# Last feed-forward stage by block products: seven products in place of eight for six of its eight chunks

## What is computed

```
h2 = rmsnorm_2(x, norm_mlp_g[l])
up = jnp.square(jax.nn.relu(jnp.einsum('bsd,df->bsf', h2, w_up[l])))     # 1024 -> 4096
x = x + jnp.einsum('bsf,fd->bsd', up, w_down[l])                         # 4096 -> 1024
```

## Time and profile before

| what | us |
|---|---|
| median of 3 runs | 996.32 (995.89 to 996.4) |
| span of the profiled execution, first to last instruction | 994.1 |
| PE busy | 987.6 (99%) |
| DVE busy | 682.7 (69%) |
| ACT busy | 553.6 (56%) |
| POOL busy | 118.6 (12%) |

### The profile page before, as it was taken

The page is one execution under the profiler, slowest core; times in us unless marked ns, Lnnn a source line. Parts: engine busy times, 40 slices in busy tenths (PEclk is TensorE's granted clock), DMA queues, the critical chain, the costliest instruction groups (busy, mean ns, idle before and its releaser), DMA issues.

```text
span 994.1 us, 12539 instructions
## 1 busy us (share of the span) xinstructions
PE 987.6 (99%) x4608; PEld 810.6 (82%) x4608; DVE 682.7 (69%) x998; ACT 553.6 (56%) x761; POOL 118.6 (12%) x109
## 2 busy tenths in 40 slices
PE   8999999999999999999999999999999999999998
PEld 7788888888777788888888888888888888888887
DVE  6666566668987667656565678776689767656663
ACT  7444343577665546444444586868885555443542
POOL 0000000022300000000000041169904000000000
PEclk9999999999999999999999999999999999999999
DMA  7987776586444546766666487658555546777761
GB/s 263 284 266 255 234 250 211 193 305 196 140 152 143 169 130 214 227 198 214 211 204 226 156 229 237 176 163 212 151 191 196 202 156 204 228 223 227 226 198 43
DMA packets 165465, 201.44 MB, mean 203 GB/s; under 512 B 55969, under 2 KB 111658, under 8 KB 165290
## 3 DMA queue, kind: packets, MB, share of 16 engines
q1 hardware_dynamic: 164826, 200.69, 64.3%
q10 hardware_dynamic: 592, 0.14, 0.1%
HBM read 182.45 MB, written 5.77 MB: 189 GB/s over the span
## 4 chain that ended last, share of the span: by engine, by line
PE 96%; DVE 2%; ACT 1%; POOL 1%; issue 0%; ACTq 0%; POOLq 0%; DVEq 0%
PE bank L1969 23%; PE bank L1971 23%; PE bank L1970 23%; PE bank L2087 7%; PE bank L2086 7%; PE bank L2085 7%; PE bank L1984 1%; PE bank L2136 1%; PE bank L2251 1%; DVE lo L1348 0%; PE bank L2151 0%; PE bank L2138 0%; PE bank L2374 0%; PE bank L2375 0%; PE bank L2347 0%
## 5 line engine op out<-in xcount | busy, mean ns | idle before, releaser
L1969 PE MATMUL bank<-hi,xh 128*128 128x512 f32 (+1 forms) x944 | 374.8, 397 | 0.9 <-DVE lo L1574 0.8
L1971 PE MATMUL bank<-hi,xl 128*128 128x512 f32 (+1 forms) x944 | 367.2, 389 | 0.0
L1970 PE MATMUL bank<-lo,xh 128*128 128x512 f32 (+1 forms) x944 | 366.5, 388 | 0.0
L1331 DVE TENSOR_TENSOR lo<-raw,hi 128x2048 fp32r<-128x2048 f32 (+1 forms) x111 | 253.9, 2289 | 146.2 <-ACT hi L824 146.2
L824 ACT ACTIVATE hi<-raw 128x2048 fp32r<-128x2048 f32 (+1 forms) x114 | 216.5, 1901 | 133.7 <-PE bank L2087 97.0
L1969 PEld LDWEIGHTS bank<-hi,xh 128*128 128x128 f32 x944 | 177.3, 188 | 39.7 <-issue 2.5
L1971 PEld LDWEIGHTS bank<-hi,xl 128*128 128x128 f32 x944 | 177.2, 188 | 37.2
L1970 PEld LDWEIGHTS bank<-lo,xh 128*128 128x128 f32 x944 | 177.5, 188 | 34.4
L1348 DVE TENSOR_TENSOR lo<-raw,hi 128x1024 fp32r<-128x1024 f32 (+1 forms) x108 | 131.9, 1230 | 43.1 <-ACT hi L833 42.4
L2085 PE MATMUL bank<-hi,hh 128*128 128x512 f32 (+1 forms) x306 | 119.3, 390 | 0.0
L2087 PE MATMUL bank<-hi,hl 128*128 128x512 f32 (+1 forms) x306 | 118.7, 388 | 0.0
(11 more groups left out here) (271 smaller groups left out, 961.6 us busy)
## 6 DMA issues: line engine op xcount, KB each, us to landing
raw<-in_w_in SPq DMA_DIRECT2D x48, 1024.0 KB
raw<-in_ffn_w_gu SPq DMA_DIRECT2D x82, 512.0 KB
raw<-in_ffn_w_down SPq DMA_DIRECT2D x22, 1024.0 KB
raw<-in_w_up SPq DMA_DIRECT2D x16, 1024.0 KB
raw<-in_w_down SPq DMA_DIRECT2D x16, 1024.0 KB
raw<-in_w_out SPq DMA_DIRECT2D x8, 1024.0 KB
distance_table<-ftab SPq DMA_DIRECT2D x8, 576.0 KB
raw<-in_w_proj_attn SPq DMA_DIRECT2D x4, 1024.0 KB
```

The costliest lines, as they stand in the source:

```text
L1331: nc.vector.tensor_tensor(lo[s][:, :, 0:width], raw[s][:, :, 0:width], hi[s][:, :, 0:width].bitcast(F32), ALU.subtract).then_inc(lo_done, 1)
L1969: nc.tensor.matmul(o, sh, wh, start=first and j == 0, stop=False)
L1970: nc.tensor.matmul(o, sh, wl, start=False, stop=False)
L1971: ins = nc.tensor.matmul(o, sl, wh, start=False, stop=last and j == 3)
```

## The change

Chunks 0 and 1 are computed as before, but one directly after the other, chunk 1 into the banks X[0] and X[1]. Chunks 2 to 7 are taken as three pairs. In a pair, the up product is a 2x2 block product: rows are the two token tiles, the inner dimension is two halves of 512, and columns are the two chunks of the pair. It is computed in seven block products (`p1` to `p7`) of one unit and 12 matmuls each, where before there were four up units of 24. The formula needs sums of blocks on both sides:

- Four sums of the input, made once by POOL in `xn` (four of 128x512, after two adds of 128x1024 that rebuild the input from `xh` and `xl`), and split by ACT and DVE into `sum_h`, `sum_l`.
- Four sums of weight blocks per pair (`weight_sums`, t = 1 to 4), each one POOL instruction on 128x2048 numbers. The weights of a pair are loaded into `operand` buffers of their own, outside the ring's `raw` buffers; `hi` and `lo` are still the ring of three.
- PSUM results are kept by ACT (`keep`), further products are added onto the same bank, and DVE adds the rest (`add_product`, three per pair). The squares go to ACT (`square`). The transposes of the last chunk go by DMA as all others.

The order of PE's work in a pair is one table; "a0" to "b1" are the four down units of earlier chunks:

```diff
-UNITS = U_L + 4 * NF2
+NPAIR = (NF2 - 2) // 2
+PRODUCTS = ["p1", "p2", "a0", "p6", "a1", "p7", "p5", "b0", "p4", "p3", "b1"]
+U_PAIR = U_L + 4
+UNITS = U_PAIR + len(PRODUCTS) * NPAIR + 4
+OPERAND = {"p1": 0, "p2": 1, "p6": 5, "p7": 2, "p5": 4, "p4": 1, "p3": 3}
...
+            def last_operand(j, b):
+                half, chunk = b % 2, 2 + 2 * j + b // 2
+                if j == 0:
+                    sp_eng.wait_ge(k_rl, 2)
+                else:
+                    sp_eng.wait_ge(lo_done, product_unit(j - 1, ("p1", "p4", "p7", "p3")[b]) + 1)
+                    sp_eng.wait_ge(last.t_made, 4 * j - (3, 0, 1, 1)[b])
...
             for c in range(4):
                 for half in range(2):
                     columns(a["w_proj_attn_2" if c < 2 else "w_proj_rnn_2"], U_P2 + 2 * c + half, c % 2 * W, half)
+                    if (c, half) in ((2, 1), (3, 1)):
+                        last_operand(0, 2 * (c - 2))
...
+            for j in range(NPAIR):
+                i = 2 + 2 * j
+                if j < NPAIR - 1:
+                    last_operand(j + 1, 0)
+                last_down(i - 1, 1)
+                last_down(i, 0)
+                flip_last(i, 0, 2 * i + 1)
+                if j < NPAIR - 1:
+                    last_operand(j + 1, 2)
+                    last_operand(j + 1, 1)
+                last_down(i, 1)
+                flip_last(i, 1, 2 * i + 2)
+                if j < NPAIR - 1:
+                    last_operand(j + 1, 3)
...
+            def weight_sums(j, which):
+                def sum_up(t, left, right, op):
+                    pool.wait_ge(last.t_made, 4 * j + t - 1)
+                    nc.gpsimd.tensor_tensor(operand[(4, 5, 2, 1)[t - 1]][:, :, :], operand[left][:, :, :],
+                                            operand[right][:, :, :], op).then_inc(last.t_made, 1)
...
+            weight_sums(0, (1, 2, 3))
             norm_rstd(4)
...
+            weight_sums(0, (4,))
+            for j in range(1, NPAIR):
+                weight_sums(j, (1, 2, 3, 4))
```

DVE's part of a pair, new:

```diff
+                for j in range(NPAIR):
+                    last_split_lo(product_unit(j, "a0"))
+                    add_product(j, 0)
+                    last_split_lo(product_unit(j, "p6"))
+                    last_split_lo(product_unit(j, "a1"))
+                    last_merge(2 * j + 1)
+                    pair_planes(j, 0)
+                    last_split_lo(product_unit(j, "p7"))
+                    last_lo(2 * j + 1)
+                    last_split_lo(product_unit(j, "p5"))
+                    last_split_lo(product_unit(j, "b0"))
+                    last_split_lo(product_unit(j, "p4"))
+                    add_product(j, 1)
+                    last_split_lo(product_unit(j, "p3"))
+                    last_split_lo(product_unit(j, "b1"))
+                    pair_planes(j, 1)
+                    last_split_lo(product_unit(j, "b1") + 1)
+                    add_product(j, 2)
+                    last_merge(2 * j + 2)
+                    pair_planes(j, 2)
+                    last_split_lo(product_unit(j, "b1") + 2)
+                    pair_planes(j, 3)
+                    last_lo(2 * j + 2)
```

More of the change, by code:

```diff
@@ L192, in __init__, with own @@
         self.merged = sem(name + "_merged")
-        self.tr = sem(name + "_tr")
+    def own(self, sem, name):
+        self.g0 = sem(name + "_g0")
+        self.acted = sem(name + "_acted")
         self.hh = sem(name + "_hh")
@@ L922, in ffn_iter @@
                 split_hi(n + 4, off)
[L923 to L924 removed]
+                split_hi(n + 5, off)
             def ffn(f, width=lambda n: W):
@@ new lines, in ffn, with last_split_hi @@
+                norm(f.norm + 1, third_unit, lambda: None)
+            def last_split_hi(n):
+                if n >= UNITS:
+                    return
+                s = n % RING
+                name = PRODUCTS[(n - U_PAIR) % len(PRODUCTS)]
+                j = (n - U_PAIR) // len(PRODUCTS)
+                if j < NPAIR and name in OPERAND:
+                    if name in ("p1", "p2", "p3"):
+                        act.wait_ge(last.b_in[OPERAND[name]], 16 * j + 16)
+                    else:
+                        act.wait_ge(last.t_made, 4 * j + ("p5", "p6", "p7", "p4").index(name) + 1)
+                else:
+                    r = [r for r in range(U_PAIR, U_PAIR + 2 * NF2) if slot_unit(r) == n][0]
+                    act.wait_ge(raw_in[r % RING], UNIT_IN * (r // RING + 1))
+                act.wait_ge(used, n - 2)
+                nc.scalar.activation(hi[s][:, :, :], whole(n)[:, :, :], ACT.Copy).then_inc(hi_done, 1)
@@ new lines, in sum_hi, with keep @@
+            def sum_hi(m):
+                act.wait_ge(last.x_made, (3, 5, 4, 6)[m - 1])
+                cut = slice(4 * (m - 1), 4 * m)
+                nc.scalar.activation(sum_h[:, cut, :], x_block[m], ACT.Copy).then_inc(last.s_hi, 1)
+            def keep(j, k):
+                act.wait_ge(used, product_unit(j, ("p1", "p6", "p7")[k]) + 1)
+                if j == 0 and k == 0:
+                    act.wait_ge(last.s_lo, 4)
+                elif j > 0:
+                    act.wait_ge(last.planes, 4 * j + (1, 4, 3)[k])
+                nc.scalar.activation((c11, c12, c22)[k], G[0][:, :], ACT.Copy).then_inc(last.kept, 1)
@@ new lines, in square @@
+            def square(j, k):
+                c = (c11, c21, c22, c12)[k]
+                rstd = rstd_x[:, 0:1] if k in (0, 3) else rstd_x[:, 1:2]
+                if k == 1:
+                    act.wait_ge(used, product_unit(j, "p4") + 1)
+                    if j > 0:
+                        act.wait_ge(last.planes, 4 * j + 2)
+                    nc.scalar.activation(c, G[0][:, :], ACT.Relu, scale=rstd).then_inc(last.acted, 1)
+                    act.wait_ge(last.acted, 4 + j + 1)
+                else:
+                    act.wait_ge(last.added, 3 * j + (1, 0, 2, 3)[k])
+                    step(nc.scalar.activation(c, c, ACT.Relu, scale=rstd))
+                nc.scalar.activation(c, c, ACT.Square).then_inc(last.squared, 1)
@@ new lines, in last_ffn @@
+            def last_ffn():
+                ffn_first(last)
+                second_chunk()
+                for j in range(NPAIR):
+                    for name in PRODUCTS:
+                        if name in OPERAND:
+                            product(j, name)
+                        else:
+                            last_down(2 * j + "ab".index(name[0]), int(name[1]))
+                for i in (NF2 - 2, NF2 - 1):
+                    for b in range(2):
+                        last_down(i, b)
```

733 lines of the change are left out of this document (479 added, 254 removed).

## The result

The changed kernel takes 1060.91 us (median of 4 runs, 1054.94 to 1062.55), the kernel before 996.21. The ratio is 1.064, 95% interval 1.0612 to 1.0668. The profiled execution has a span of 1060.7 us.

What follows compares the result with a forecast made beforehand. PE, busy 99% of the span, was taken to bound the kernel. Span 994.1 less 9.0 of saved PE work plus 55.9 of waits gave 1041.0; the median lies 2.2 above, so 1043 us, range 998 to 1056.

Steps and rivals of the forecast that it cites:

- 1, late load of U_P2+6: Output projections: this unit's load is issued behind one waiting for `k_rl`, so PE waits; +3.5 us.
- 2, sums at the output projections: Output projections: POOL's t1 falls in slack, t2 and t3 of pair 0 hit the turned `otl`; 2 us taken.
- 3, chunks 0 and 1: Before a0 of pair 0: DVE's 19.2 us of work plus 13.8 inserted by POOL outlast PE's cover; +12.7 us.
- 4, pair ends: Two pair ends: three POOL sums (t2, t3, t4) enter DVE's queue; +14.7 us each, 29.4 in all.
- 5, t1 beside b0: Next pair's first weight sum runs beside the split of b0, which has 5.44 us of cover; +2.4 us twice, 4.8.
- 6, after the last pair: After the last pair no p1 and p2 cover DVE's chain of planes, split and low part; +3.5 us.
- Q: Time of one POOL sum of 128x2048, charged in DVE's queue: 4.6 us taken, between 4.4 and 5.8.
- the walk: Place-by-place count of waits; for chunks 0 and 1, DVE from 823.3 to 856.3 until a0 of pair 0 can run.
- The clock falls in the gaps: Rival: three PE gaps of 9 to 13 us each followed by a half-clock unit, 5.4 us each; about 1059; chance 0.05.
- long instructions of both engines run side by side: Rival: DVE and POOL overlap on long instructions, leaving 10.3 to 18.1 us of waits; 998 to 1005; chance 0.15.
- The 16-number row: A 3.90 us POOL instruction on 16 numbers, in whose last 0.56 us a DVE split took its undisturbed 1.23.
- Faster: Rival: PE's waits sum to less than 9.0 us, so time falls, to 987 at no wait; chance 0.10.

Runs made afterwards that it cites:

- fill experiment: The changed kernel with 174 idle matmuls into the unused bank X[1], written ahead of the waits where PE stands idle: 1050.02 us.
- free sums: The changed kernel with weight and input sums on POOL cut to 4 columns and the first operand loads of pair 0 issued later: 996.32 us.

## Why the prediction was wrong, step by step

The direction was right, and the time lay 5 us above the range. The gaps of PE, each from the end of one matmul's 0.227 us to the start of the next in PE's timeline, against the terms of the sum:

| step | forecast | measured |
|---|---|---|
| 1, late load of U_P2+6 | 3.5 | 4.7 |
| 2, sums at the output projections | 2 | 4.9 (2.4, 0.7, 1.8) |
| 3, chunks 0 and 1 | 12.7 | 9.7 (3.0, 6.7) |
| 4, pair ends | 29.4 | 27.6 (13.8 twice) |
| 5, t1 beside b0 | 4.8 | 6.0 (3.2, 2.8) |
| 6, after the last pair | 3.5 | 3.5 |
| sum | 55.9 | 56.4 |

**The cost of POOL's sums was right, and so were the places.** That the sums of the table agree within 0.5 us is luck in part: single steps are off by up to 3 us, both ways. Q = 4.6 was right: 4.62 us for a sum that DVE barely disturbed. Step 2 was too low since I named `otl`, where the sums hit `xn` and the gates as well. Step 3 was too high by 3.0. In the trace DVE takes 31.2 us from the planes at 837.86 to the end of a0's split at 869.10, where the walk had 33.0, and some 1.6 more are covered by PE itself, whose matmuls ran slow from 857.9 to 861.3. Its 3.0 us before p2 are the input sums' doing: they stay with the weight sums on few columns (2.8 in the list of waits) and are gone when the input sums are small too. Step 4 put 14.7 at each pair end and got 13.8: the sums hit the planes and the two low parts, 13.0 us in place of three times 4.6, and the split of p2 escaped. Step 5's 2.4 doesn't come out of its terms: a sum paid in full gives 1.91 + 2.29 + 4.6 - 5.44 = 3.4, which is nearer to the 3.2 and 2.8 measured.

**The step that failed is the clock.** I set the span as 994.1 - 9.0 + 55.9, every matmul at 0.227 us, and gave "The clock falls in the gaps" 0.05. Measured, 985.1 + 56.4 is 1041.5, and the span is 1060.7; 19 us are matmuls at the lower level. The granted clock says the same by itself: nine stretches at 0.5 lie behind the eleven gaps, PE works in about 37 us of them, and half of that is 18. That is the whole miss. The chance was the error: I took the absence of a lower clock in a trace whose longest wait is 1.8 us as evidence for gaps of 13 us, of which it says nothing. The price, 5.4 us for each of three gaps, was also built wrong. Behind the long gaps the matmuls of 4.9 us ran slow, which loses half of that, about 2.5; but nearly every gap had it, those of 3 us too. The window from 880 to 900, whose one gap is 3.2 us, has a granted clock of 0.91; the gap of 1.8 at 806 had no such stretch. So nine stretches cost about 2 us each, and not three 5.4. That this rival's time, about 1059, lies 2 us from the measured one is luck: 3 x 5.4 is 16.2, and 9 x 2.1 is 19. The fill experiment took 10.9 us out by this alone, down to 1050.0, inside the range. The Trainium skill, "TensorE: Matmul & The Clock Gate", section "Part 1: The HAM clock gate", has the halving of an idle PE, and this trace agrees (0.54 and 0.51 in the windows at 922 to 936.5); I cited it and then left it out of the sum.

**The rivals.** That long instructions of both engines run side by side is refuted by the sums on few columns, by one sum twice, and by the 5.08 and 9.90 us rows. The 16-number row of POOL, on which it rested, is one case in which DVE didn't wait. That such an instruction lets DVE through because it reads next to nothing, and has read it by then, is argued, not shown. The forecast for that rival, 998 to 1005 with steps 1 and 6 in place, was also a little low: the experiment with sums on few columns, input sums and late load in place, has 1009.4, and the one without these 996.3. "Faster" had its point at 9.0 us of stall in total; even with free sums the stalls and their clock make about that much (996.3, where 987.2 is the time before less 9.0).

**Open.** The runs of the changed kernel scatter by 7.6 us (1054.94 to 1062.55), those of the kernel before by 0.5; the mean clocks of the four runs (0.976 for the fastest, 0.971 for the slowest) suggest that it is the length of the slow stretches that varies, but what sets it in a run was not tried. Nor is a gap's price the same each time: behind the last gap of 3.5 us the changed kernel lost 1.7 us and the version with free sums 3.0, and in the fill experiment a gap of 3.0 at 854 had none (granted clock 1.00 from 850 to 862).

## What to carry to other kernels

Before work is given to an idle POOL, look at what DVE reads at that moment: a long POOL instruction that reads SBUF beside DVE's two-input instructions or its 16-bit copies has to be costed in DVE's queue, in full, at whichever of these is next there. If it must be, cut it into short pieces; that alone gave back 24 of 65 us here. Saved matmuls on a PE that never waits are worth their time only while no gap arises, and here a gap of about 3 us or more mostly cost some 2 us more than its own length, in matmuls at the lower clock; a forecast has to have both in its sum.

## What the runs showed of the hardware

- POOL memsets of 128x2048 (1.81 us) didn't slow DVE's tensor_tensor of the same size (2.28), but a DVE 16-bit copy, 1.35 us alone, took 2.38 beside them, and two memsets there took 5.33 in place of 3.70. The Trainium skill, "SBUF — State Buffer", section "SBUF: two separate sides", has a two-input DVE instruction contend only with POOL instructions that read SBUF, and one in a 2-port mode with any. The tensor_tensor row agrees. The copy's does if the copy runs in such a mode, which no row names.
- A DVE instruction with one input in SBUF and one in PSUM isn't held up: `xn<-xn,bank` on 128x512 took its 0.68 us at 912.13 in the run with one-input instructions, beside a POOL instruction that ran from 910.15 to 913.96. POOL waits for DVE in turn: that instruction took 3.81 in place of about 2.2.
- A POOL tensor_tensor on 128x2048 takes 4.6 us where DVE leaves it alone, one on 128x512 takes 1.28, and a tensor_scalar on 128x2048 1.9 to 2.2.
- Filling a gap with matmuls whose result nobody reads made the kernel 10.9 us faster.
